# Two weight remainders on VectorE, one round ahead of where they were made

## The chip, the cores and the metric

The kernel runs on one core of a Trainium2 chip. The metric is device time of one execution in microseconds (us); the kernel before takes 2344.04 us, the median of 3 runs (2343.74 to 2344.35).

## The reference, cut to what matters

Two blocks, one after the other, work on 256 tokens of width 1024. Each block is an attention part and then an expert part ("peer") with 16384 experts, of which each token takes 16 for each of 8 heads:

```python
u_sel = jnp.take(u_tab, idx, axis=0)
h = jnp.einsum('bthkd,btd->bthk', u_sel, xb)
a = (jax.nn.gelu(h.astype(jnp.float32)) * g).astype(xb.dtype)
return jnp.einsum('bthk,bthkd->btd', a, jnp.take(v_tab, idx, axis=0))
```

All is float32. The change concerns the last line alone, the product of the gated activations with the table `v`.

## The kernel before, in words

The kernel takes no experts out of the tables. It computes all 16384 activations of all tokens (the u products), multiplies them by a gate matrix that is zero for experts not chosen, and multiplies the result by the whole table v (the v products, "expert output products"). Both tables, and all other weights, stream through a ring of four buffers, `ring[:, 0..3]`; one slot is 128x1024 float32 (512 KB). 32 rounds of four slots are one table.

A float32 product is made of three products at the fast rate (`split_product`, lines 489 to 491): high by high, high by remainder, remainder by high. So each operand is split in a rounded part and a remainder:

- ScalarE makes the rounded weights, `high` (line 962, `whi[:, j]` from `ring[:, j]`), when the slot has landed and TensorE has used the same buffer in the round before (`slot_used`).
- The weight remainder `wlo = ring - whi` is made by GpSimd (line 446, all four places in most stages) or by VectorE (`low`, line 1436). In the second half of the v rounds GpSimd has places 0 and 2, and VectorE places 1 and 3 (`DVE_PLACES = (1, 3)`). Either counts up `lo_ready[j]`, for which TensorE waits before slot j, and SyncE before it loads the buffer anew (line 424, in the order 0, 1, 2, 3, one queue).
- The activations of two slots are a pair. ScalarE makes the rounded pair `shi` in `left` (line 991), VectorE the remainder `slo` in `rest_of` (line 1430). There are two buffers of each, one for places 0 and 1 and one for places 2 and 3. TensorE waits for `pair_ready` before places 0 and 2.

TensorE's `v_round` (line 763) takes for each slot two token tiles by two column halves by three products: 12 matmuls of 512 columns. ScalarE's `v_round` (line 1008) makes, for round k, the high of place 0 and of place 1 of round k+1, the left of the first pair of round k+1, the high of places 2 and 3, the left of the second pair. Each high waits until TensorE has used that place in round k.

The rounds 0 to 15 are gated: between them TensorE also makes gate tiles (line 730) and VectorE multiplies them into `act` (`apply`, line 1411). The gates are then done, and rounds 16 to 31 are ungated: VectorE has only `low` and `rest_of`. Before these it and ScalarE both wait for the last gate product (`gates_used`). VectorE's order there is written by hand (lines 1442 to 1456): the two `rest_of` of round 16, and then for each round k and each c of 0 and 1, `low(k, place)` and `rest_of` of pair c of round k+1. The last two `low` stand alone. All this happens twice, once in each block.

Of the kernel before, what the change touches and what calls it, by code (L numbers as in the profile page):

```python
# [64 lines left out]
ROUNDS = E_TILES // RING  # L65
Q_TILES = 2 * HEADS
HALF = NKEY // 2
HALF_ROUND = ROUNDS // 2
# [6 lines left out]
POOL_PLACES, DVE_PLACES = (0, 2), (1, 3)  # L75
# [75 lines left out]
def block_program(nc, weights, const1, const2, gains, keys_in, x, out):  # L151
    with ExitStack() as ctx:
# [897 lines left out]
        def _(eng):  # L1050
# [286 lines left out]
            def experts(b):  # L1337
# [89 lines left out]
                def rest_of(p, j):  # L1427

                    eng.wait_ge(n["shi_ready"], p + 1)
                    eng.tensor_tensor(slo[:, j, :, :], act[:, bass.ds(p * 2, 2), :], shi[:, j, :, :].bitcast(F32), ALU.subtract)\  # L1430
                       .then_inc(n["pair_ready"], 1)

                def low(k, j):

                    eng.wait_ge(hi_ready[j], k + (first_v // RING + 1))
                    eng.tensor_tensor(wlo[:, j, :], ring[:, j, :], whi[:, j, :].bitcast(F32), ALU.subtract)\  # L1436
                       .then_inc(lo_ready[j], 1)
# [10 lines left out]
                    apply(last_k, c, GROUPS, 1, c)  # L1448
                eng.wait_ge(n["gates_used"], 2 * GROUPS)
                for c in range(2):  # L1450
                    rest_of(2 * last_k + 2 + c, c)
                with eng.Fori(HALF_ROUND, ROUNDS - 1) as k:
                    for c in range(2):
                        low(k, DVE_PLACES[c])
                        rest_of(k * 2 + (2 + c), c)
                for c in range(2):
                    low(ROUNDS - 1, DVE_PLACES[c])
                eng.wait_ge(n["acc_ready"], 1)
                for a in range(4):
                    c = slice((a % 2) * 512, (a % 2 + 1) * 512)  # L1460
# [7 lines left out]
            attention1()  # L1468
            norm(1)
            experts(0)  # L1470
            norm(2)
            attention2()
            norm(3)
            experts(1)
            eng.wait_ge(fin_sq, TT)
            eng.tensor_scalar(stat[:, 1, 0:TT], stat[:, 0, 0:TT], 1.0 / D, EPS, ALU.mult, ALU.add).then_inc(fin_var, 1)
# [101 lines left out]
```

## Time and profile before

| | |
|---|---|
| median of 3 runs | 2344.04 us |
| the profiled execution's own time | 2348.5 us |
| its span, first to last instruction | 2346.7 us |
| mean granted TensorE clock | 0.967 of full speed |
| TensorE matmul busy | 2104.7 us (90%) |
| VectorE, ScalarE, GpSimd busy | 53%, 42%, 63% |
| ungated half of the v products, block 1 | 1007.2 to 1239.7 us of the span |
| ungated half of the v products, block 2 | 2099.4 to 2332.5 us of the span |

Times in the profile count from the start of the span. PE is TensorE, PEld its weight load, DVE VectorE, ACT ScalarE, POOL GpSimd, SPq the DMA issues of SyncE. A matmul's row is longer than the distance to the next row, since matmuls are pipelined; the distance between starts is the pace.

### The profile page before, as it was taken

To read this page: it belongs to the slowest core of one execution; us is meant where nothing else is said; L and a number is where in the kernel's file an instruction comes from. 1 tells how busy PE (TensorE), PEld (TensorE's weight loads), DVE (VectorE), ACT (ScalarE), POOL (GpSimd) and SP (SyncE) were. 2 spreads that over 40 slices of the span, in tenths; PEclk is the share of its full clock that TensorE was granted. 3 is DMA by queue.
4 is the path that set the end of the run, shared out by engine and by line. 5 is a ranking of instruction groups with operands and counts; after the bars stand their busy time and mean duration, and the time that the engine had idled before them with its cause. 6 is when DMAs were issued, how large, how long until landed. Compare 5 with 4: busy or idle time off the path is not lost.

```text
span 2346.7 us, 41347 instructions
## 1 busy us (share of the span) xinstructions
PE 2104.7 (90%) x15340; PEld 1900.9 (81%) x15340; DVE 1237.0 (53%) x2076; ACT 976.1 (42%) x1206; POOL 1474.5 (63%) x592
## 2 busy tenths in 40 slices
PE   6898889999999999978887988998999999987886
PEld 6797789999999877756666978998999977776664
DVE  5547539971455567622224744994155556652222
ACT  3356334444444344333335454444444344433332
POOL 5654656897777688733335535798777768853332
PEclk9898899999999999999998989999999999999999
DMA  5332334554545455533445324455455545533432
GB/s 214 126 126 91 118 121 140 179 177 163 172 167 165 148 170 170 169 116 143 143 143 197 108 79 135 153 170 178 161 165 166 169 144 172 169 133 143 143 143 107
DMA packets 95823, 351.93 MB, mean 150 GB/s; under 512 B 11024, under 2 KB 11280, under 8 KB 95376
## 3 DMA queue, kind: packets, MB, share of 16 engines
q1 hardware_dynamic: 94752, 345.92, 43.7%
q10 hardware_dynamic: 1008, 5.13, 0.6%
q8 instruction: 45, 0.74, 0.1%
q14 instruction: 18, 0.15, 0.0%
HBM read 349.96 MB, written 1.05 MB: 150 GB/s over the span
## 4 chain that ended last, share of the span: by engine, by line
PE 58%; DVE 16%; DMA 9%; issue 7%; ACT 5%; POOL 4%; DVEq 0%; ACTq 0%; SPq 0%; POOLq 0%; PEldq 0%
PE ps L489 18%; PE ps L490 17%; PE ps L491 17%; DMA ring<-in_weights 9%; POOL wlo L446 4%; DVE wlo L1436 3%; PE ps L730 3%; ACT shi L991 2%; DVE work L1347 1%; ACT whi L962 1%; DVE work L1334 1%; PE ps L656 1%; DVE work L1327 1%; DVE work L1328 1%; DVE act L1171 0%
## 5 line engine op out<-in xcount | busy, mean ns | idle before, releaser
L446 POOL TENSOR_TENSOR wlo<-ring,whi 128x1024 fp32r<-128x1024 f32 x588 | 1474.3, 2515 | 844.4 <-ACT whi L962 609.0
L962 ACT ACTIVATE whi<-ring 128x1024 fp32r<-128x1024 f32 x536 | 565.0, 1059 | 980.4 <-PE ps L491 701.9
L489 PE MATMUL ps<-hhi,whi 128*128 128x256 f32 x2432 | 701.5, 288 | 16.4 <-POOL wlo L446 15.2
L490 PE MATMUL ps<-hlo,whi 128*128 128x256 f32 x2432 | 692.4, 285 | 0.0
L491 PE MATMUL ps<-hhi,wlo 128*128 128x256 f32 x2432 | 691.9, 285 | 0.0
L489 PE MATMUL ps<-whi,shi 128*128 128x512 f32 x1024 | 421.1, 411 | 104.1 <-DVE wlo L1436 85.1
L489 PEld LDWEIGHTS ps<-hhi,whi 128*128 128x128 f32 x2432 | 470.9, 194 | 19.8 <-issue 11.6
L490 PEld LDWEIGHTS ps<-hlo,whi 128*128 128x128 f32 x2432 | 471.1, 194 | 0.0
L491 PEld LDWEIGHTS ps<-hhi,wlo 128*128 128x128 f32 x2432 | 470.3, 193 | 0.0
L490 PE MATMUL ps<-wlo,shi 128*128 128x512 f32 x1024 | 409.5, 400 | 0.0
L491 PE MATMUL ps<-whi,slo 128*128 128x512 f32 x1024 | 408.3, 399 | 0.0
L489 PEld LDWEIGHTS ps<-whi,shi 128*128 128x128 f32 x1024 | 195.3, 191 | 172.2 <-DVE wlo L1436 111.2
L1411 DVE TENSOR_TENSOR act<-ps,act 128x512 f32 (+1 forms) x128 | 88.5, 692 | 404.7 <-PE ps L730 404.7
L1430 DVE TENSOR_TENSOR slo<-act,shi 128x512 fp32r<-128x512 f32 x128 | 91.7, 718 | 338.8 <-ACT shi L991 338.8
L491 PEld LDWEIGHTS ps<-whi,slo 128*128 128x128 f32 x1024 | 195.2, 191 | 47.0
L490 PEld LDWEIGHTS ps<-wlo,shi 128*128 128x128 f32 x1024 | 195.5, 191 | 41.6
L489 PE MATMUL ps<-whi,hhi 128*128 128x256 f32 x704 | 207.5, 295 | 15.5 <-DVE hlo L1084 11.0
L490 PE MATMUL ps<-wlo,hhi 128*128 128x256 f32 x704 | 204.1, 290 | 0.0
L491 PE MATMUL ps<-whi,hlo 128*128 128x256 f32 x704 | 203.5, 289 | 0.0
L489 PEld LDWEIGHTS ps<-whi,hhi 128*128 128x128 f32 x704 | 140.5, 200 | 19.9 <-issue 14.7
L1401 DVE TENSOR_TENSOR work<-iota,ps 128x1024 f16<-128x1024 f16 x128 | 155.5, 1215 | 0.0
L490 PEld LDWEIGHTS ps<-wlo,hhi 128*128 128x128 f32 x704 | 140.3, 199 | 0.0
(241 smaller groups left out, 2017.1 us busy)
## 6 DMA issues: line engine op xcount, KB each, us to landing
ring<-in_weights SPq DMA_DIRECT2D x652, 512.0 KB, 3.3
act<-in_const SPq DMA_DIRECT2D x1, 2752.0 KB, 14.0
act<-in_const ACTq DMA_DIRECT2D x1, 2372.0 KB, 10.2
xres<-in_x SPq DMA_DIRECT2D x2, 512.0 KB, 4.3
act<-in_keys ACTq DMA_DIRECT2D x1, 1024.0 KB, 13.8
out<-act ACTq DMA_DIRECT2D x2, 512.0 KB, 2.6
act<-in_fgain ACTq DMA_DIRECT2D x1, 512.0 KB, 3.5
act<-in_keys SPq DMA_DIRECT2D x1, 128.0 KB, 13.8
```

The lines of the kernel that those rows point to most:

```text
L446: pool.tensor_tensor(wlo[:, j, :], ring[:, j, :], whi[:, j, :].bitcast(F32), ALU.subtract)\
L489: pe.matmul(dst, wide[0], narrow[0], start=start, stop=False, skip_group_check=True)
L490: pe.matmul(dst, wide[0], narrow[1], start=False, stop=False, skip_group_check=True)
L491: return pe.matmul(dst, wide[1], narrow[0], start=False, stop=stop, skip_group_check=True)
L656: mm = pe.matmul(bank(6 + t, h * P, (h + 1) * P), kl[:, h, t, :], ql[:, h, t, :], start=True, stop=True)
L730: mm = pe.matmul(bank(6 + c, q * HALF, (q + 1) * HALF), hot2[:, c, q, :], hot1[:, c, w, q, :], start=(q + w == 0), stop=(w == 1), skip_gro ...
L962: eng.activation(whi[:, j, :], ring[:, j, :], ACT.Copy).then_inc(hi_ready[j], 1)
L991: eng.activation(shi[:, j, :, :], act[:, bass.ds(p * 2, 2), :], ACT.Copy).then_inc(n["shi_ready"], 1)
L1401: eng.tensor_tensor(hot2[:, j], iota[:, :].unsqueeze(1).to_broadcast([P, TOK, NKEY]), over(row(1, at), NKEY), ALU.is_equal)
L1411: eng.tensor_tensor(a, bank(6 + j).rearrange("p (q k) -> p k q", q=TOK), a, ALU.mult)\
L1430: eng.tensor_tensor(slo[:, j, :, :], act[:, bass.ds(p * 2, 2), :], shi[:, j, :, :].bitcast(F32), ALU.subtract)\
L1436: eng.tensor_tensor(wlo[:, j, :], ring[:, j, :], whi[:, j, :].bitcast(F32), ALU.subtract)\
```

## The change

In the ungated half, `low` of both places moves one round ahead: the two of round 16 are made before the loop, each ahead of a `rest_of` of round 16, and in the loop `low(k + 1, place)` stands where `low(k, place)` stood. The two at the end go. The number of instructions and what they compute are the same.

```diff
                 eng.wait_ge(n["gates_used"], 2 * GROUPS)
                 for c in range(2):
+                    low(HALF_ROUND, DVE_PLACES[c])
                     rest_of(2 * last_k + 2 + c, c)
                 with eng.Fori(HALF_ROUND, ROUNDS - 1) as k:
                     for c in range(2):
-                        low(k, DVE_PLACES[c])
+                        low(k + 1, DVE_PLACES[c])
                         rest_of(k * 2 + (2 + c), c)
-                for c in range(2):
-                    low(ROUNDS - 1, DVE_PLACES[c])
                 eng.wait_ge(n["acc_ready"], 1)
```

## Rows read from the trace of the kernel before

**Rows 1.** Windows: two full-pace stretches (u, gated v), then the two ungated halves.

```profile
core 0: us, PE busy (x) PEld busy (x) DVE busy (x) ACT busy (x) POOL busy (x), PEclk, DMA share, GB/s
560.00:600.00 40.00, 40.00 (x335) 40.00 (x335) 0.00 (x0) 18.00 (x21) 33.52 (x14) 1.00 0.56 184
880.00:920.00 40.00, 40.00 (x255) 31.80 (x254) 28.32 (x41) 16.96 (x20) 31.87 (x14) 1.00 0.51 170
1007.20:1239.70 232.50, 189.50 (x768) 143.62 (x768) 58.96 (x63) 83.12 (x95) 84.48 (x34) 0.99 0.42 147
2099.40:2332.50 233.10, 191.00 (x768) 144.85 (x768) 58.97 (x63) 79.98 (x92) 77.30 (x31) 0.98 0.38 135
```

**Rows 2.** Waits of the first ungated half: who for whom, us, times, longest.

```profile
ACT whi L962 <- DMA ring<-in_weights: 117.1, 29, 4.3
PE ps L489 <- DVE wlo L1436: 43.0, 30, 1.8
PE ps L489 <- DVE slo L1430: 5.1, 1, 5.1
```

**Rows 3.** Timeline of one ungated round, all engines: start, length, what, idle before.

```profile
1069.08 1.22 DVE L1436 TENSOR_TENSOR wlo<-ring,whi 128x1024 fp32r<-128x1024 f32 x1
1070.46 8.63 SPq L424 DMA_DIRECT2D ring<-in_weights  x4
1074.15 1.06 ACT L962 ACTIVATE whi<-ring 128x1024 fp32r<-128x1024 f32 x1 [4.04 <-DMA ring<-in_weights]
1075.12 0.61 ACT L991 ACTIVATE shi<-act 128x512 fp32r x1
1075.90 0.69 DVE L1430 TENSOR_TENSOR slo<-act,shi 128x512 fp32r<-128x512 f32 x1 [5.61 <-ACT shi L991]
1076.51 1.22 DVE L1436 TENSOR_TENSOR wlo<-ring,whi 128x1024 fp32r<-128x1024 f32 x1
1077.79 0.50 PE L489 MATMUL ps<-whi,shi 128*128 128x512 f32 x1 [1.58 <-DVE wlo L1436]
1083.62 1.22 DVE L1436 TENSOR_TENSOR wlo<-ring,whi 128x1024 fp32r<-128x1024 f32 x1
```

**Rows 4.** Timeline of TensorE: the last unbroken run of the second half.

```profile
2324.37 0.40 PE L490 MATMUL ps<-wlo,shi 128*128 128x512 f32 x1
...
2332.30 0.40 PE L491 MATMUL ps<-whi,slo 128*128 128x512 f32 x1
```

**Rows 5.** Timeline of the first ungated half's start, all engines.

```profile
1002.14 0.69 DVE L1411 TENSOR_TENSOR act<-ps,act 128x512 f32<-128x512 f32 x1 [5.47 <-PE ps L730]
1003.10 2.00 ACT L962 ACTIVATE whi<-ring 128x1024 fp32r<-128x1024 f32 x2 [12.19 <-DVE act L1411]
1004.24 5.13 POOL L446 TENSOR_TENSOR wlo<-ring,whi 128x1024 fp32r<-128x1024 f32 x2 [11.36 <-ACT whi L962]
1005.73 1.41 DVE L1430 TENSOR_TENSOR slo<-act,shi 128x512 fp32r<-128x512 f32 x1 [2.90 <-ACT shi L991]
1007.19 0.80 PE L489 MATMUL ps<-whi,shi 128*128 128x512 f32 x1 [5.09 <-DVE slo L1430]
1008.07 1.85 DVE L1430 TENSOR_TENSOR slo<-act,shi 128x512 fp32r<-128x512 f32 x1 [0.94 <-ACT shi L991]
1012.41 0.39 PE L489 MATMUL ps<-whi,shi 128*128 128x512 f32 x1
```

**Rows 6.** Windows at that start (columns as in the first group).

```profile
1006.00:1010.00 4.00, 2.81 (x7) 2.23 (x8) 3.06 (x3) 2.04 (x3) 3.31 (x2) 0.50 0.35 131
```

**Rows 7.** Timeline elsewhere: VectorE and GpSimd want SBUF at once.

```profile
242.35 1.50 DVE L1184 TENSOR_TENSOR act<-act 128x384 f32<-128x384 f32 x1 [0.66 <-ACT act L886]
243.39 2.66 POOL L446 TENSOR_TENSOR wlo<-ring,whi 128x1024 fp32r<-128x1024 f32 x1
243.77 3.44 DVE L1103 CAST whi<-ring 128x1024 fp32r<-128x1024 f32 x2
```

**Rows 8.** Timeline just after the first gate products end: ScalarE, then GpSimd.

```profile
1012.61 1.06 ACT L962 ACTIVATE whi<-ring 128x1024 fp32r<-128x1024 f32 x1 [4.57 <-PE ps L491]
1013.75 2.40 POOL L446 TENSOR_TENSOR wlo<-ring,whi 128x1024 fp32r<-128x1024 f32 x1 [4.37 <-ACT whi L962]
```

**Rows 9.** DMA issues of the first ungated half: count, KB, median us to landing.

```profile
ring<-in_weights SPq DMA_DIRECT2D x65, 512.0 KB, 3.9
```

## The prediction, made before the changed kernel was run

> **What bounds the kernel now.** I read the stage windows first. In the ungated u rounds and in the gated v rounds TensorE is busy 40.00 of 40.00 us; in the two ungated v halves only 189.5 of 232.5 and 191.0 of 233.1 us [rows 1]. So only there has TensorE idle time to give back. The waits of that stretch then name the releaser: 30 times TensorE waits for VectorE's weight remainder, and almost as often (29 times, 117.1 us) ScalarE waits for the ring's DMA [rows 2]. GpSimd, whose remainders serve places 0 and 2, holds TensorE up nowhere in that list.
>
> The timeline of one round shows how the two belong together [rows 3]. VectorE ends the remainder of place 1 (from 1069.08); only then may the buffer be loaded again (1070.46 is the issue). ScalarE, which takes its work in order, waits 4.04 us for that load, makes the high at 1074.15 and the rounded pair at 1075.12; VectorE was waiting for that pair (5.61 us idle), makes its remainder at 1075.90, and only behind it, at 1076.51, the weight remainder of place 3, for which TensorE waits until 1077.79. The same follows with places changed, and ends at 1083.62. The half-rounds are 1076.51 - 1069.08 = 7.43 and 1083.62 - 1076.51 = 7.11 us, 14.54 us a round. It is a closed chain of latencies: remainder, load, high, pair, pair's remainder, next remainder. The weights of place 3 had long been there; their remainder stood behind a pair of the next round.
>
> **TensorE's own pace.** From 2324.37 to 2332.30 there are 34 steps: 7.93 / 34 = 0.2333 us a matmul [rows 4], over slot borders too. A slot of 12 is 2.80 us, a half-round 5.60, a round 11.20 us. The first slot after the gates is slower: 1012.41 - 1007.19 = 5.22 us for 12 matmuls [rows 5], at a granted clock of 0.50, the lower of the two levels (1.2 GHz), after 5.1 us without work [rows 5, 6]. So the stage at TensorE's pace would be 5.22 + 756 x 0.2333 = 181.6 us. It takes 232.5 and 233.1 [rows 1]: 50.9 and 51.5 us of it are stalls (about 1.7 for each of the 30 waits [rows 2]; the view books 1.4, since a matmul's row outlasts its step by 0.16 and the first after a gap starts more slowly, 0.50 instead of 0.40).
>
> **The change, part by part.** *Removed: the wait of place 1 and place 3 for VectorE.* The low of place 1 of round k+1 now needs only its high, which needs place 1 of round k used and the load landed. From rows: ScalarE starts a high at 1012.61, and the remainder after it starts at 1013.75, 1.14 us later [rows 8]. Counted from the end of slot (k, 0) at TensorE's pace: GpSimd's remainder runs from 1.2 to 3.6; slot (k, 1) ends at 2.8, VectorE's low runs from 4.0 to 5.2 and the pair's remainder until 5.8; slot (k, 2) ends at 5.6, GpSimd 6.8 to 9.2; slot (k, 3) ends at 8.4, VectorE 9.6 to 11.4. The first pair of round k+1 is wanted at about 11 and ready at 5.8; the remainder of place 1 is wanted at about 13.6 and ready at 5.2. Slack is 5 us or more, three times the present stall.
>
> *Moved: the loads.* The buffer of place 1 is free at 5.2, the load is issued and lands some 3.9 us later [rows 9], at about 9.5, and is wanted by ScalarE at 14.0. A buffer's own loop is high 1.06, remainder 2.40 at most, load 3.9, handovers under 1: about 8 us of the 11.2 that a round will last. SyncE's queue takes 0, 1, 2, 3, which is the order in which the buffers come free. No DMA is added; the rate rises from 147 GB/s by 232.5/181.6 to 188 GB/s, and the ungated u rounds run at 184 with TensorE never idle [rows 1]. I take 0 for it; that cover gone, the bound from below is 0 and from above the wait that now stands there (rival 1).
>
> *Moved behind the low: the pair's remainder.* In steady state it is 1.2 us later with 5 us of slack, so 0. At the start of the stage it is not covered. TensorE starts when the remainder of the first pair of round 16 is there (it ends at 1007.14) [rows 5], and now the low of place 1 comes ahead. Three rows show what that meets: VectorE's 0.69 us subtraction took 1.41 and 1.85 us there, and each ended about 0.5 us after a GpSimd remainder did (the first of the two GpSimd pieces, 2.40 us, ended at 1006.64, the second at 1009.37) [rows 5]. One waits for the other's end. The Trainium skill, SBUF — State Buffer, section on the two separate sides, says so: VectorE with two SBUF inputs and GpSimd hold a shared port pair exclusively, for a whole instruction. By that rule, which the trace agrees with, the new first instruction costs more than its own 1.22 us here. From rows: the low is ready at 1005.2, gets in at 1006.64 as the subtraction did, and ends 0.53 later than it, at 1007.67. GpSimd's second piece has then been waiting; elsewhere such a waiting GpSimd piece (from 243.39) went ahead of VectorE's next instruction, whose two pieces took 3.44 us [rows 7]. So it runs 2.23 us to 1009.90, and the pair's remainder ends 0.55 later at 1010.45: TensorE starts 3.3 us later. If VectorE keeps its turn, it is 1007.67 + 0.61 = 1008.28, 1.1 us later; the low bound is 0. I take 3.3 (that row is the same contest), in each block. Clock at the start: 5.22 us for the first slot again, taken as it is.
>
> *Removed at the end:* the two lows behind the last pair; their saving is in the stalls counted. The 2.5 us of final additions and everything after shift as a whole.
>
> Sum: 50.9 + 51.5 - 2 x 3.3 = **95.8 us**. Against the profiled execution: span 2346.7 - 95.8 = 2250.9, its own time 2348.5 to 2252.7. The runs' median stands 4.5 below that own time, so 2344.04 - 95.8 = **2248.2 us**. Bounds of the known terms: start cost 0 gives 2241.6, and leftover stalls of 0.2 us a half-round (62 of them) give 2260.6.
>
> **The rivals.** *1. A part of the stalls stays.* The reload or a collision of VectorE with GpSimd holds the chain: the distance between GpSimd's end (3.6) and VectorE's start (4.0) is only 0.4 us. For it: VectorE's operations do double when they meet [rows 5]. Against: a meeting costs VectorE some 2.4 us at most where 5 are free, and the loads have 4. Price: worked at its worst, two meetings in each half-round, 1.14 + (2.4 + 1.1) + (2.4 + 0.55) = 7.6 us from slot to pair where two slots last 5.6: a round of 13.2 instead of 14.54, a gain of 1.34 x 16 x 2 = 43 and a time of 2301. The same page's exclusive hold is what this case would rest on; two meetings in each half-round cannot be had with one GpSimd piece there. Chance 0.08 for something between 2262 and 2335.
>
> *2. The wait only moves.* ScalarE waits for the DMA 29 times [rows 2]; were the loads themselves late, TensorE would wait for the same loads through GpSimd's places: 2344. Against: the loads are late because they are issued late (1070.46, behind the low). Chance 0.03.
>
> *3. Slower.* TensorE without gaps is given the lower clock in this stage. At the lower level a slot took 5.22 us instead of 2.80, so a stage of all slots there lasts 334 us and the point of no gain is where 21 of its 64 slots run so (20.9 x 2.42 = 50.9 - 0.3). At half the slots: 32 x 2.42 = 77 - 51 = 26 in each block, 2397 us. Against: the gated half before it, as dense, has clock 1.00 [rows 1]. Chance 0.02.
>
> **How the numbers follow.** Forecast (2240 to 2262) 0.87, rival 1 0.08, rival 2 0.03, rival 3 0.02. The range 2240 to 2262 takes in the start's bounds and small leftover stalls, and leaves out the rivals, 0.13 together. A measurement tells about 0.2% (4.7 us): faster by more 0.95, within 0.03, slower 0.02.
>
> **What would show it.** In the profile after: the ungated windows about 182 us of matmuls with TensorE idle under 2 us behind the start; no wait of line 489 for line 1436; ScalarE's waits in the loop for TensorE, not for the DMA; VectorE's low starting about 1.2 us behind each high of places 1 and 3; at the start TensorE beginning some 3 us later, with GpSimd's second piece between VectorE's low and its pair. The prediction is wrong if TensorE still waits in each half-round (rival 1, and the releaser says which), if the DMA's landing grows so much that ScalarE still waits for it (2), or if the granted clock in the stage falls under 1 for long (3).

## The result, and the profile after

The changed kernel takes 2250.34 us (median of 4 runs, 2239.26 to 2251.81), the kernel before beside it 2344.19: a ratio of 0.959 (95% interval 0.9566 to 0.9613). Of the four runs of the kernel before three took 2343.74 to 2344.35 us and one 5168.11, for a reason that no trace here shows. The prediction was 2248.2 us in 2240 to 2262. The profiled execution takes 2250.24 us, its span is 2248.5 (before 2346.7).

The waits of the first ungated half after the change (who for whom, us in total, times, longest):

```profile
DVE wlo L1436 <- ACT whi L962: 119.5, 31, 7.7
POOL wlo L446 <- ACT whi L962: 99.9, 30, 7.2
ACT whi L962 <- PE ps L491: 95.5, 60, 7.9
PE ps L489 <- DVE slo L1430: 8.4, 1, 8.4
```

Against [rows 2]: TensorE waited 30 times for VectorE's weight remainder; now it waits once, at the start of the half, and for the first pair. ScalarE waited 29 times for the ring's DMA; now only for TensorE. ScalarE waits for TensorE, and VectorE and GpSimd wait for ScalarE: the engines follow TensorE, which no longer waits for any of them in the loop.

The windows from TensorE's first ungated matmul to just behind its last, in both blocks (columns as in [rows 1]):

```profile
1008.20:1190.00 181.80, 181.77 (x768) 145.33 (x768) 56.51 (x62) 82.35 (x93) 78.42 (x33) 0.99 0.56 185
2052.60:2234.50 181.90, 181.83 (x768) 146.06 (x768) 56.54 (x62) 79.26 (x90) 72.20 (x30) 0.99 0.51 169
```

TensorE is busy all the time; 232.5 and 233.1 us [rows 1] have become about 181.8. The DMA moved 185 and 169 GB/s where it had moved 147 and 135. The timeline of a half-round and a little more, without TensorE and the loads:

```profile
1061.28 1.06 ACT L962 ACTIVATE whi<-ring 128x1024 fp32r<-128x1024 f32 x1 [1.74 <-PE ps L491]
1062.24 0.62 ACT L991 ACTIVATE shi<-act 128x512 fp32r x1
1062.37 1.23 DVE L1436 TENSOR_TENSOR wlo<-ring,whi 128x1024 fp32r<-128x1024 f32 x1 [3.77 <-ACT whi L962]
1063.52 0.68 DVE L1430 TENSOR_TENSOR slo<-act,shi 128x512 fp32r<-128x512 f32 x1
1064.08 1.06 ACT L962 ACTIVATE whi<-ring 128x1024 fp32r<-128x1024 f32 x1 [1.22 <-PE ps L491]
1065.21 2.40 POOL L446 TENSOR_TENSOR wlo<-ring,whi 128x1024 fp32r<-128x1024 f32 x1 [3.20 <-ACT whi L962]
1066.88 1.06 ACT L962 ACTIVATE whi<-ring 128x1024 fp32r<-128x1024 f32 x1 [1.74 <-PE ps L491]
1067.97 1.23 DVE L1436 TENSOR_TENSOR wlo<-ring,whi 128x1024 fp32r<-128x1024 f32 x1 [3.77 <-ACT whi L962]
```

Compare this with [rows 3]. There ScalarE's high came after 4.04 us of idle time, ended by the DMA; here it comes after 1.74 us, ended by TensorE. VectorE's low starts 1.09 us after ScalarE's high does, and the period is 1067.97 - 1062.37 = 5.60 us, TensorE's own half-round. GpSimd's piece (1065.21 to 1067.61) ends 0.36 us before VectorE's starts, so the two do not meet. From 1014 us on, behind the start, all 30 lows of VectorE in this half take 1.23 us and all 30 pair remainders 0.68: none of them is held up.

The start of the half, on all engines:

```profile
999.88 0.69 DVE L1411 TENSOR_TENSOR act<-ps,act 128x512 f32<-128x512 f32 x1 [5.47 <-PE ps L730]
1001.99 5.64 POOL L446 TENSOR_TENSOR wlo<-ring,whi 128x1024 fp32r<-128x1024 f32 x2 [11.36 <-ACT whi L962]
1002.96 2.47 DVE L1436 TENSOR_TENSOR wlo<-ring,whi 128x1024 fp32r<-128x1024 f32 x1 [2.38 <-ACT whi L962]
1005.35 2.83 DVE L1430 TENSOR_TENSOR slo<-act,shi 128x512 fp32r<-128x512 f32 x1
1008.23 0.80 PE L489 MATMUL ps<-whi,shi 128*128 128x512 f32 x1 [8.38 <-DVE slo L1430]
1013.48 0.39 PE L489 MATMUL ps<-whi,shi 128*128 128x512 f32 x1
```

From the start of the last gate product (line 1411) to TensorE's start it was 1007.19 - 1002.14 = 5.05 us [rows 5] and is 1008.23 - 999.88 = 8.35. VectorE's low takes 2.47 us in place of 1.22, the pair's remainder 2.83 in place of 0.69: each ends behind a GpSimd piece (the group of two ends at 1007.63, the pair's remainder 0.55 us later). The first slot takes 1013.48 - 1008.23 = 5.25 us at the lower clock, as before (5.22).

To compare kernels without what happens elsewhere, I measure a block from the start of its last gate product to the start of its final additions (line 1461 before, 1460 after). Before: 1240.00 - 1002.14 = 237.9 and 2332.83 - 2094.37 = 238.5 us. After: 1190.17 - 999.88 = 190.3 and 2234.60 - 2044.30 = 190.3. So the change gives 95.7 us (47.57 + 48.16). The spans differ by 98.2; 2.3 of the rest lie ahead of the first ungated half (999.88 against 1002.14), where both programs are the same.

### The profile page after: what moved, and what is told of

The parts are those of the page before. It is cut to its first block, busy times and chain, and to the rows that moved or that the text cites. A ratio compares the mean times of both kernels' runs of the same rounds, so it can differ in the third digit from the quotient of the medians.

```text
span 2248.5 us, 41347 instructions
## 1 busy us (share of the span) xinstructions
PE 2084.5 (93%) x15340; PEld 1900.6 (85%) x15340; DVE 1239.6 (55%) x2076; ACT 976.5 (43%) x1206; POOL 1469.6 (65%) x592
## 4 chain that ended last, share of the span: by engine, by line
PE 76%; DVE 13%; POOL 4%; ACT 3%; issue 3%; DMA 1%; ACTq 0%; POOLq 0%; DVEq 0%; SPq 0%; PEldq 0%
PE ps L489 24%; PE ps L490 23%; PE ps L491 23%; POOL wlo L446 4%; PE ps L730 3%; DVE work L1347 1%; DVE work L1334 1%; PE ps L656 1%; DVE work L1327 1%; DVE work L1328 1%; DVE act L1171 1%; DVE whi L1103 1%; DVE act L1126 0%; DMA act<-in_const 0%; DVE act L1117 0%
## 5 line engine op out<-in xcount | busy, mean ns | idle before, releaser
L489 PE MATMUL ps<-hhi,whi 128*128 128x256 f32 x2432 | 701.1, 288 | 16.7 <-POOL wlo L446 15.3
L489 PE MATMUL ps<-whi,shi 128*128 128x512 f32 x1024 | 413.8, 404 | 25.6 <-DVE slo L1430 25.6
L1436 DVE TENSOR_TENSOR wlo<-ring,whi 128x1024 fp32r<-128x1024 f32 x64 | 80.9, 1264 | 238.9 <-ACT whi L962 238.9
```

What stands on the lines that cost most here:

```text
L489: pe.matmul(dst, wide[0], narrow[0], start=start, stop=False, skip_group_check=True)
```

## The experiments

All edits are on the changed kernel. Each "block" is the distance just defined, in block 1 and block 2; the total is the median.

**again.** The same kernel once more.

> The changed kernel once more, as the yardstick of the variants that differ from it by a few us. Theory (stalls were VectorE's order; start cost 3.3 us a block): 2250 us again, 94 below before. Rival (part of the 94 us was a property of that run): anything further than 3 us from 2250.

Measured: 2245.93 us (6 runs, 2237.92 to 2252.28), the kernel before beside it 2344.01 (11 runs, 2334.91 to 2351.43), ratio 0.959 (0.9563 to 0.9616). Blocks 190.2 and 190.2 us. The gain holds, 98 us by these medians. But the median is 4 us from the 2250 that was expected, where the rival had set its mark at 3: the totals of one kernel spread more than the expectation allowed for. The block distances don't: 190.3 and 190.3 in the profiled run after the change, 190.2 and 190.2 in this one. Where the spread lies, the windows from 60 to 120 us tell, in the first attention part, first of the run after the change and then of this one:

```profile
60.00:120.00 60.00, 51.72 (x368) 50.10 (x369) 33.56 (x21) 20.89 (x31) 39.91 (x16) 0.89 0.37 125
```

```profile
60.00:120.00 60.00, 54.01 (x407) 52.27 (x408) 34.58 (x25) 25.96 (x38) 43.86 (x18) 0.94 0.43 141
```

The clock was 0.89 there in one execution and 0.94 in the other, and TensorE began 407 matmuls instead of 368. The last gate product of block 1 starts at 991.09 here and at 999.88 there. So 9 of the 12.4 us between these two spans arise before the changed code is reached; for terms of a few us I go by the block.

**pair_first.** The pair's remainder ahead of the low, before the loop only.

```diff
                 for c in range(2):
-                    low(HALF_ROUND, DVE_PLACES[c])
                     rest_of(2 * last_k + 2 + c, c)
+                    low(HALF_ROUND, DVE_PLACES[c])
```

> Only the two lines ahead of the loop change places: the remainder of the first pair of round 16 comes before the weight remainder of place 1; in the loop nothing changes. Theory (that weight remainder, and the GpSimd piece that goes ahead of the pair while it waits, delay TensorE's start by 3.3 us in each block): TensorE starts 5.1 us after the last gate product's start in place of 8.35, time 2250.3 - 6.6 = 2243.7 us. Rival (the start is bound by GpSimd's own remainder of place 0, or the delay only moves to the second slot): 2248 to 2251.

Measured: 2240.71 us (5 runs, 2234.44 to 2243.33), ratio 0.9553 (0.9528 to 0.9578), where 2243.7 was expected; blocks 186.9 and 187.0 us, 3.3 less each than after the change, as expected. The timeline at the start:

```profile
999.73 0.69 DVE L1411 TENSOR_TENSOR act<-ps,act 128x512 f32<-128x512 f32 x1 [5.47 <-PE ps L730]
1003.32 1.42 DVE L1430 TENSOR_TENSOR slo<-act,shi 128x512 fp32r<-128x512 f32 x1 [2.90 <-ACT shi L991]
1004.66 3.39 DVE L1436 TENSOR_TENSOR wlo<-ring,whi 128x1024 fp32r<-128x1024 f32 x1
1004.79 0.80 PE L489 MATMUL ps<-whi,shi 128*128 128x512 f32 x1 [5.10 <-DVE slo L1430]
```

TensorE starts 5.06 us after the last gate product, as before the change. The low, now behind the pair, takes 3.39 us: again GpSimd's waiting piece went first, but now in front of something that TensorE wants only a slot later. So the start cost of 3.3 us comes from the order of these two instructions, and it can be had back without touching the gain in the loop.

**highs_early.** As pair_first, and ScalarE makes the four highs of round 16 ahead of its wait for the gates. The diff shows ScalarE's part alone.

```diff
                 with eng.Fori(0, HALF_ROUND - 1) as k:
                     v_round(k)
+                for j in range(RING):
+                    high(first_v + j + RING, j, HALF_ROUND - 1)
                 eng.wait_ge(n["gates_used"], 2 * GROUPS)
-                with eng.Fori(HALF_ROUND - 1, ROUNDS - 1) as k:
+                for c in range(2):
+                    left(2 * HALF_ROUND + c, c)
+                with eng.Fori(HALF_ROUND, ROUNDS - 1) as k:
                     v_round(k)
```

> As pair_first, and ScalarE makes the four rounded weights of round 16 before it waits for the last gate product, not behind it. Theory (the start is a chain gate product, two highs of 2.0 us, rounded pair 0.61, pair's remainder 0.69, with the GpSimd pieces in its way): the chain loses 2.0 us and the meeting with GpSimd (0.7), so TensorE idles about 2.5 us in place of 5.1, and the time is 2243.7 - 2 x 2.6 = 2238.5 us; if the shorter gap also leaves the clock at its upper level, another 2.4 us a block, 2233.7. Rival (highs are not on that chain): 2243.7.

Measured: 2235.48 us (5 runs, 2228.98 to 2238.37), ratio 0.9534 (0.9509 to 0.956); blocks 183.3 and 183.3 us, 3.6 less each than pair_first, 7.0 less than after the change. By blocks and by medians it is the fastest of all kernels here. (Lines behind the inserted ones have numbers 4 higher: 1434 is `rest_of`.)

```profile
1001.78 0.69 DVE L1415 TENSOR_TENSOR act<-ps,act 128x512 f32<-128x512 f32 x1 [5.47 <-PE ps L730]
1003.24 0.69 DVE L1434 TENSOR_TENSOR slo<-act,shi 128x512 fp32r<-128x512 f32 x1 [0.77 <-ACT shi L991]
1003.99 0.50 PE L489 MATMUL ps<-whi,shi 128*128 128x512 f32 x1 [2.24 <-DVE slo L1434]
```

TensorE is idle for 2.24 us instead of 5.1, which is 2.9 of the 3.6 us. The windows there show what became of the clock:

```profile
1000.00:1004.00 4.00, 1.76 (x23) 1.23 (x21) 1.45 (x3) 2.21 (x3) 2.08 (x1) 1.00 0.00 0
1004.00:1008.00 4.00, 4.00 (x12) 3.14 (x13) 2.80 (x3) 0.00 (x0) 0.00 (x0) 0.64 0.38 138
```

It still falls (0.64, from 1.00), although only 2.24 us were idle and TensorE was already at work again; but the lower level lasts less long. The 13th matmul shows it, the first of the second slot, in pair_first and here:

```profile
1009.98 0.39 PE L489 MATMUL ps<-whi,shi 128*128 128x512 f32 x1
```

```profile
1008.36 0.46 PE L489 MATMUL ps<-whi,shi 128*128 128x512 f32 x1
```

The first slot takes 1009.98 - 1004.79 = 5.19 us there and 1008.36 - 1003.99 = 4.37 here, 0.8 us less. With the 2.9 us this is the gain of 3.6 to 0.1 us; of the 2.4 us hoped for from the clock, 0.8 came.

**gpsimd_all.** GpSimd makes all four weight remainders also in the ungated half.

```diff
-                lows(first, first + HALF_ROUND, POOL_PLACES)
+                lows(first, first + HALF_ROUND, range(RING))
...
                 for c in range(2):
-                    low(HALF_ROUND, DVE_PLACES[c])
                     rest_of(2 * last_k + 2 + c, c)
                 with eng.Fori(HALF_ROUND, ROUNDS - 1) as k:
                     for c in range(2):
-                        low(k + 1, DVE_PLACES[c])
                         rest_of(k * 2 + (2 + c), c)
```

> In the ungated half GpSimd makes all four weight remainders, VectorE only those of the pairs. Theory (the stall was VectorE's order, and GpSimd has room for four pieces of 2.40 and two holds of 0.6 us, 10.8 of 11.2 us a round): TensorE's pace holds, and the start has no low in front of the pair, 2244 to 2250 us. Rival (the share of VectorE is needed since GpSimd and VectorE collide): TensorE waits for line 446, 12 us a round or more, 2270 us or more.

Measured: 2239.75 us (4 runs, 2231.07 to 2245.79), ratio 0.9559 (0.9524 to 0.9593); blocks 187.0 and 187.0 us, the same as pair_first to 0.1 us. The total lies 4 us under the range of 2244 to 2250, for which the totals' spread is enough.

```profile
1057.10 2.40 POOL L446 TENSOR_TENSOR wlo<-ring,whi 128x1024 fp32r<-128x1024 f32 x1 [0.39 <-ACT whi L962]
1057.69 2.36 DVE L1430 TENSOR_TENSOR slo<-act,shi 128x512 fp32r<-128x512 f32 x1 [3.24 <-ACT shi L991]
1059.90 2.40 POOL L446 TENSOR_TENSOR wlo<-ring,whi 128x1024 fp32r<-128x1024 f32 x1 [0.40 <-ACT whi L962]
1062.70 2.40 POOL L446 TENSOR_TENSOR wlo<-ring,whi 128x1024 fp32r<-128x1024 f32 x1 [0.40 <-ACT whi L962]
1063.31 2.34 DVE L1430 TENSOR_TENSOR slo<-act,shi 128x512 fp32r<-128x512 f32 x1 [3.26 <-ACT shi L991]
```

GpSimd starts a piece every 2.80 us, a slot's time, with 0.40 us to spare. And VectorE's pair remainder takes 2.34 to 2.36 us instead of 0.69 in every half-round: it meets GpSimd each time, and in the loop TensorE never waits. The pair that is ready at 1057.69 + 2.36 = 1060.05 is wanted with a slot that starts at 1061.36, so 1.3 us are left. A meeting in each half-round therefore costs nothing here. Two things follow. VectorE's share of the weight remainders was not needed at all; in the order of before it only cost. And one meeting in each half-round, at its full price, does not hold TensorE up.

**lows_together.** Both lows of round k, then both pairs of round k+1, and the lead of a round taken back. Put the other way, it is the kernel before with one line added, `for c in range(2):` between `low` and `rest_of`.

```diff
                 for c in range(2):
-                    low(HALF_ROUND, DVE_PLACES[c])
                     rest_of(2 * last_k + 2 + c, c)
                 with eng.Fori(HALF_ROUND, ROUNDS - 1) as k:
                     for c in range(2):
-                        low(k + 1, DVE_PLACES[c])
+                        low(k, DVE_PLACES[c])
+                    for c in range(2):
                         rest_of(k * 2 + (2 + c), c)
+                for c in range(2):
+                    low(ROUNDS - 1, DVE_PLACES[c])
```

> Half of the change: in the loop both weight remainders of round k come first and then both pair remainders of round k+1, so only place 3 is freed from standing behind a pair; nothing is made a round ahead. From the start of the last gate product to the final additions a block took 237.9 us before and 190.3 after. Theory (every stall is VectorE's order, a chain of handovers): place 1 still stands behind the pair of places 2 and 3: high, pair, pair's remainder, low, about 3.6 us from the use of place 3 where TensorE has 2.4, so one stall of about 1.2 us a round instead of two of 1.7; the start as before the change (3.3 us less than after): 190.3 - 3.3 + 16 x 1.2 = 206 us a block, 2282 us in all. Rival A (what counts is the full round of lead, half of it brings nothing): 238 and 2344. Rival B (only the alternation with the pairs hurt): 187 and 2244.

Measured: 2271.4 us (2 runs), ratio 0.9688 (0.9632 to 0.9745); blocks 203.6 and 203.7 us, 16.7 over the 187.0 of pair_first, whose start it has. TensorE's waits in the first block:

```profile
PE ps L489 <- DVE wlo L1436: 12.8, 15, 0.9
PE ps L489 <- DVE slo L1430: 5.1, 1, 5.1
```

15 stalls instead of 30, of 16.7 / 15 = 1.1 us instead of 1.7. The block was forecast at 206; the total came out 11 below its forecast of 2282, of which 5 are the two blocks and the rest is within the totals' spread. Neither rival's time is near. The order alone, with the same work and the same DMAs, gives two thirds of the gain (34 us a block, from 237.9 to 203.6, of the 51 from 237.9 to pair_first's 187.0).

**place1_only.** The lead for place 1, place 3 in its own round.

```diff
-                for c in range(2):
-                    low(HALF_ROUND, DVE_PLACES[c])
-                    rest_of(2 * last_k + 2 + c, c)
+                low(HALF_ROUND, DVE_PLACES[0])
+                for c in range(2):
+                    rest_of(2 * last_k + 2 + c, c)
                 with eng.Fori(HALF_ROUND, ROUNDS - 1) as k:
-                    for c in range(2):
-                        low(k + 1, DVE_PLACES[c])
-                        rest_of(k * 2 + (2 + c), c)
+                    low(k + 1, DVE_PLACES[0])
+                    rest_of(k * 2 + 2, 0)
+                    low(k, DVE_PLACES[1])
+                    rest_of(k * 2 + 3, 1)
+                low(ROUNDS - 1, DVE_PLACES[1])
```

> The change for place 1 alone; place 3 is made in its own round, behind the first pair of the next. Theory: place 3's remainder comes behind high, low of place 1, pair's remainder, about 4.2 us from the use of place 1 where TensorE has 2.5, so one stall of about 1.7 us a round: 190.3 + 16 x 1.7 = 217 us a block, 2304 us in all; the stalls stand at place 3 alone. Rival (the stall is the closed chain of load and remainder over both places, and breaking it at one place frees both): 190 to 195 and 2250 to 2260.

Measured: 2306.25 us (2 runs), ratio 0.9837 (0.9777 to 0.9897); blocks 221.8 and 220.4 us: 31.6 and 30.1 over after the change, 2.0 to 2.1 for each of the 15 stalls where 1.7 was expected. The stalls stand at place 3 alone, one a round; the rival is out. The timeline shows some of TensorE's restarts, and where the rest is:

```profile
1045.64 0.50 PE L489 MATMUL ps<-whi,shi 128*128 128x512 f32 x1 [1.34 <-DVE wlo L1436]
1059.05 0.50 PE L489 MATMUL ps<-whi,shi 128*128 128x512 f32 x1 [1.95 <-DVE wlo L1436]
1073.40 0.50 PE L489 MATMUL ps<-whi,shi 128*128 128x512 f32 x1 [1.34 <-DVE wlo L1436]
1086.21 0.50 PE L489 MATMUL ps<-whi,shi 128*128 128x512 f32 x1 [1.35 <-DVE wlo L1436]
```

The plain round is 1086.21 - 1073.40 = 12.81 us, a stall of 12.81 - 11.20 = 1.61, where 1.7 was computed. At 1059.05 the wait was 0.6 longer, and the round behind it 14.35 long, 1.54 more than the plain one. The low ahead of that wait met GpSimd's piece, and behind the wait the clock fell:

```profile
1053.77 2.41 POOL L446 TENSOR_TENSOR wlo<-ring,whi 128x1024 fp32r<-128x1024 f32 x1 [5.90 <-ACT whi L962]
1055.43 1.83 DVE L1436 TENSOR_TENSOR wlo<-ring,whi 128x1024 fp32r<-128x1024 f32 x1 [3.69 <-ACT whi L962]
```

```profile
1059.00:1062.00 3.00, 2.95 (x9) 2.39 (x10) 0.00 (x0) 0.00 (x0) 2.24 (x1) 0.68 0.57 184
```

The forecast had left both out. In this block five rounds are longer by their wait (by 0.6, 0.6, 0.6, 0.9 and 0.1 us), and windows of 3 us show such falls three times. 15 x 1.61 + 2.8 + 3 x 1.54 = 31.6 us, which is the whole block. Here, where nothing is to spare, a meeting is a stall, and a stall now and then costs the clock as well.

**loads_late.** Each of SyncE's loads in the ungated half (rounds 17 to 31) waits until TensorE has used the slot that the same buffer held before. The diff shows the waits alone; the function around them is left out.

```diff
+                    for k in range(first, end):
+                        for j in range(RING):
+                            sp.wait_ge(lo_ready[j], k)
+                            sp.wait_ge(slot_used, (k - 1) * RING + j + 1)
+                            load(k, j)
```

> The changed kernel, but SyncE loads a buffer in the ungated half only when TensorE has used the slot before it, so that no load runs ahead. It prices the cover of the loads, which the prediction put at 4 us and more. Theory: a load lands 3.3 to 3.9 us after the use, high 1.06, low 1.2, pair's remainder 0.6 and handovers: the pair is ready 6.6 to 7.1 us after the use of place 1 where two slots last 5.6, so a half-round is 6.0 to 6.4 us, 13 to 26 us a block: 203 to 216 us a block, 2276 to 2302 us; ScalarE waits for the DMA. Rival (loads are never near the chain): 190 and 2250.

Measured: 2280.6 us (2 runs), ratio 0.9728 (0.9664 to 0.9791); blocks 207.6 and 207.3 us, 17 over after the change. The waits of the first block behind its first 15 us (line numbers are 17 higher here):

```profile
ACT whi L979 <- DMA ring<-in_weights: 105.9, 55, 11.4
PE ps L506 <- DVE slo L1447: 10.5, 22, 0.9
```

ScalarE waits for the DMA 55 times; TensorE now waits for the pair, 17 us in some 31 half-rounds, 0.55 each, inside the 0.4 to 0.8 expected. So with no load ahead at all the chain is only 0.55 us too long. By the schedule of the prediction the loads of the changed kernel can be issued about 9 us before ScalarE wants them (5.2 against 14.0); how much of that is to spare was not measured, but that it is enough is: ScalarE waits for no load in the loop after the change.

## Why the prediction was right, point by point

*TensorE's pace.* It put the stage at 181.6 us; the windows show TensorE at work for 181.8 in both blocks. The stalls of 50.9 and 51.5 us are gone whole.

*The steady state.* The schedule worked out from [rows 8] put VectorE's low at 4.0 us from the end of slot (k, 0), 0.4 behind GpSimd's end; the trace shows 0.36. Highs wait for TensorE, not for the DMA, as listed. lows_together and place1_only, priced with the same handovers at 1.2 and 1.7 us a stall, measured 1.1 and 1.6 (2.0 to 2.1 with meetings and clock), so the mechanism is shown by parts: a remainder that TensorE wants soon stood behind one that waits for TensorE itself.

*The slack had a slip.* The prediction gave the first pair of a round until about 11 us and the remainder of place 1 until 13.6. By its own schedule slot (k, 3) ends at 8.4, so the next round's place 0 starts there and place 1 at 11.2: the pair has 8.4 - 5.8 = 2.6 us to spare and not 5, the remainder of place 1 11.2 - 5.2 = 6.0. The trace agrees: a pair is ready at 1063.52 + 0.68 = 1064.20, and its slot, the 21st of the half, starts at 1013.48 + 19 x 2.80 = 1066.68, 2.5 us later. That the term still came out at 0 is right, since the low's 1.2 us are less than 2.6; but the margin over the present stall of 1.7 was half what the text said, and gpsimd_all used up half of it.

*The loads.* Cost 0 was right; loads_late gives the price of that cover gone, 17 us a block.

*The start.* Forecast: TensorE 3.3 us later in each block, by an instruction that gets in behind GpSimd's first piece, and a pair that stands behind GpSimd's second. Measured 3.3 (8.35 - 5.05), in just that order, and pair_first takes it away again. The Trainium skill, SBUF — State Buffer, section on the two separate sides, has the two engines hold the port one at a time, for whole instructions; the traces agree with that rule: in gpsimd_all 0.69 us of VectorE's work last 2.36 beside a GpSimd piece, and end 0.55 us behind it (1060.05 against 1057.10 + 2.40).

*The sum.* 95.8 us was forecast and 95.7 measured in the blocks. The total is 2250.34 against 2248.2; the remaining 2 us are less than the runs of one kernel differ by (2237.92 to 2252.28 in one set).

*The rivals.* That a part stays (1) fell, since VectorE and GpSimd do not meet in the loop of the changed kernel, close as the 0.36 us are; a meeting once in each half-round at gpsimd_all's price, 2.36 - 0.69 = 1.7 us, would by an estimate still have fitted into the pair's 2.5 us. The prediction's price for this rival has a slip too: 7.6 us where two slots last 5.6 is 2.0 too much in each half-round, so a round of 15.2 us and not 13.2, longer than the 14.54 of before. Nothing in the forecast used that figure. That the wait only moves (2) fell with [rows 2] against the waits after. A lower clock under dense work (3) didn't come: 0.99 over the stage, with the start's low clock in it. In place1_only the clock fell behind stalls instead.

## What to carry to other kernels

On an engine that works in order, ask of every instruction what it waits for: one that waits for the bottleneck must not stand ahead of one that the bottleneck wants next, and the work that frees a transfer's buffer counts as wanted. When a step is moved ahead, look at the one place where there is no slack yet, the first round: its order can be written by hand apart from the loop's, here worth 3.3 us a block. And check whether the second engine was needed at all; here GpSimd alone kept the pace.

## What the runs showed that was not expected

- When VectorE and GpSimd both wanted to read SBUF one behind the other, the one that had waited went next in both contests seen here, even against an instruction already queued on the other: the pair's remainder of 2.83 us after the change, and the low of 3.39 us in pair_first, both stood behind a GpSimd piece that had been waiting.
- Idle time of 2.24 us was followed by a fall of the clock some 1 us after TensorE had restarted (highs_early). In place1_only three of the 15 stalls of block 1 and two of block 2 were followed by a fall, in the kernel before one of 60. The length of the wait alone doesn't tell which: in block 2 of place1_only the clock fell after waits of 1.77 and 1.78 us and not after one of 2.22.
- The same program differs by up to 14 us between executions (2237.92 to 2252.28), the kernel before by 16.5. In the two profiled executions of the changed kernel most of the difference arises in the first attention part, where the clock stays at the lower level for different lengths; the block distances repeat to 0.2 us where TensorE is not stalled in the loop.
